# Hybrid decoder step: gathers of 4 picks for 32 tokens, and a weighted sum on four 32-column groups of TensorE

## The chip, the cores and the metric

One core of a Trainium2 chip. The metric is the device time of one execution in microseconds; the unchanged kernel takes 5937.07 us (median of 3 runs).

## The reference, cut to what matters

One layer: three gated branches, then a mixer of experts ("PEER"). The change touches the mixer alone. For every token (1024 of the prompt, 32 of the sample) and each of 8 heads, two sets of 128 keys are scored, the best 16 of each are combined to 256 candidates, and the best 16 of these name 16 of 16384 experts:

```
eidx = take_along_axis(cidx, pos, axis=-1)                 # (token, head, 16)
gw   = softmax(sc, axis=-1)
hpre = einsum('td,thkd->thk', xb, u_tab[eidx])             # a dot of 1024 with a gathered row
act  = gelu(hpre) * gw
y    = h + einsum('thk,thkd->td', act, v_tab[eidx])        # weighted sum of gathered rows
```

All is float32. An expert's u row and v row lie side by side in a scratch table, so one fetch of 8 KB brings both.

## The kernel before, in words

The stages run one after another; `experts` (line 2014) is the last and takes from 3160 us to the end. It works in 9 tiles: 8 of 128 prompt tokens and one of the 32 sample tokens. A turn is one head of a tile (for the sample tile 4 heads lie side by side on the partitions, so it has 2 turns); there are 66 turns of 16 picks, 1056 picks in all.

For one pick of a prompt tile, partition p holds token p:

- GpSimd (line 2133) issues one indirect DMA: for each of 128 partitions a row of 8 KB by the index in `E`, 1 MB in all, into one of 12 slots of `rows`. It waits for `v_done`, that the weighted sum has freed the slot 12 picks before.
- VectorE, `dot` (L2307), multiplies the u half by the tile's `n2u` and sums it. After each pick it does one of 16 parts of `route` for the turn after next: the top-16 searches, with `E` at part 13 (L2290) and the gates at part 15 (L2297).
- ScalarE, `weights` and `diagonal`: gelu (L2169), times gate (L2173), and a 128 x 128 diagonal of the weights (L2181).
- TensorE, `sum_row` (L2385): two products, diagonal by 512 columns of the v half, added up in PSUM (`ps_y`, 128 x 1024, double buffered by tile). Each float32 product is two pairs of weight load and matmul in the trace. At a tile's first pick the row `h` is put in by a product with the identity (L2379).
- TensorE also does the queries of the turn 3 ahead (L2354, after pick 4), its scores (L2367, after pick 7), and transposes at a tile's start.
- SyncE loads at each tile boundary `n2r` (L2114), `n2u` (L2103, double buffered by tile; for the sample tile 4 copies of 32 rows, L2106) and `h` (L2117), and stores `yo` (L2120). Its queue works in order: a wait holds all behind it.

In the sample tile a pick's 128 rows are 4 heads of 32 tokens; `fold` (128 x 32: the identity's four blocks added) times the weights takes the diagonal's place (L2185), so that the product has 32 output rows.

Of the kernel before, what the change touches and what calls it, by code (L numbers as in the profile page):

```python
# [23 lines left out]
P = 128  # L24
D = 1024
# [1988 lines left out]
def experts(nc, d):  # L2014
# [10 lines left out]
    SLOTS = 12  # L2025
    DIAGS = 4
    LOW = -3e38

    with ExitStack() as ctx:
# [16 lines left out]
        E, gates = sb("E", [P, 4, K], u32), sb("gates", [P, 4, K])  # L2046
# [3 lines left out]
        ps_q, ps_s = pb("ps_q", [P, 512]), pb("ps_s", [P, 512])  # L2050
# [4 lines left out]
        n2u_in = [sem(f"n2u_in{i}") for i in range(2)]  # L2055
# [5 lines left out]
        E_done, ex_in, ex_out, er_done, gate_done = (sem(n) for n in ("E", "ex_in", "ex_out", "er", "gate"))  # L2061
# [22 lines left out]

        def tokens(tile):
            return slice(tile * P, tile * P + width(tile))

        @block.sync
        def _(sp):
# [9 lines left out]
            def load_u(tile):  # L2099
                if tile >= 2:  # L2100
                    sp.wait_ge(dot_done, K * first_of(tile - 1))
                if tile < NT:
                    sp.dma_start(n2u[:, tile % 2], d["n2"][tokens(tile), :]).then_inc(n2u_in[tile % 2], 16)  # L2103
                else:
                    for i in range(PACK):
                        sp.dma_start(n2u[i * NS:(i + 1) * NS, tile % 2], d["n2"][tokens(tile), :]).then_inc(n2u_in[tile % 2], 16)  # L2106

            load_u(0)
            sp.dma_start(h[:], d["h"][tokens(0), :]).then_inc(h_in, 16)
            for tile in range(TILES):  # L2110
                n = width(tile)
# [25 lines left out]
        def _(act):  # L2137
# [28 lines left out]
            def weights(turn, k):  # L2166
# [3 lines left out]
                if k == 0:  # L2170
                    act.wait_ge(gate_done, turn + 1)
                act.wait_ge(gel_done, p + 1)
                nc.scalar.mul(w[:, j, k:k + 1], gel[:, j, k:k + 1], gates[:, turn % 4, k:k + 1]).then_inc(w_done, 1)  # L2173

            def diagonal(turn, k):
# [4 lines left out]
                if turn < NT * PH:  # L2180
                    nc.scalar.mul(diag[:, p % DIAGS, :], ident[:], w[:, j, k:k + 1]).then_inc(diag_done, 1)  # L2181
                else:
                    if p == NT * PH * K:
                        act.wait_ge(fold_done, PACK)
                    nc.scalar.mul(diag[:, p % DIAGS, 0:NS], fold[:], w[:, j, k:k + 1]).then_inc(diag_done, 1)  # L2185

            def outputs(tile):
                act.wait_ge(y_sum, tile + 1)
                if tile:
                    act.wait_ge(y_stored, 16 * tile)  # L2190
                n = width(tile)
                nc.scalar.copy(yo[0:n], ps_y[0:n, tile % 2]).then_inc(y_done, 1)
# [8 lines left out]
            for turn in range(TURNS):  # L2201
                for k in range(K):
                    weights(turn, k)
                    diagonal(turn, k)
                    if turn + 3 < TURNS:
                        if k == 2 and opens(turn + 3):
# [5 lines left out]
                    if k == 3 and turn and closes(turn - 1):  # L2212
                        outputs(tile_of(turn - 1))
# [282 lines left out]
```

## Time and profile before

| | |
|---|---|
| runs | 5933.24, 5937.07, 5937.49 us; median 5937.07 |
| profiled execution | 5942.84 us, its span 5941.2 us |
| mean granted TensorE clock | 0.882 of full |
| busy: TensorE matmul, VectorE, ScalarE, GpSimd | 4848.2, 2600.4, 1804.7, 1595.2 us |
| DMA | 1640.60 MB, mean 276 GB/s; 406 to 421 GB/s in most of the experts stage |

The span runs from the first to the last instruction; 1.6 us of the execution lie around it. A line of the profile gives line, engine and operation, output<-inputs, count, and then busy us and mean ns of one. Matmul ends are modelled, so a matmul's mean (613 ns) can be longer than the distance from one to the next. Times in brackets are idle time before an instruction and what ended it.

### The profile page before, as it was taken

How to read it: one execution, taken by the hardware profiler on the slowest of the kernel's cores; microseconds unless marked ns; L12 is line 12 of the kernel's file. 1: busy time of each engine (PE TensorE's matmuls, PEld its weight loads, DVE VectorE, ACT ScalarE, POOL GpSimd, SP SyncE). 2: the span in 40 equal slices, each digit the busy share in tenths (PEclk: the TensorE clock that was granted, in tenths of full speed). 3: DMA queues.
4: the chain of work that ended last, by engine and by line, in shares of the span. 5: the costliest groups of instructions: out<-in, count | busy, mean ns of one | idle time of the engine just before them, and what ended most of it. 6: DMA issues, size and time to landing. Idle time of an engine off the chain costs nothing. (4 is left out here: it accounts for less than half of the span.)

```text
span 5941.2 us, 55349 instructions
## 1 busy us (share of the span) xinstructions
PE 4848.2 (82%) x17762; PEld 3079.4 (52%) x17762; DVE 2600.4 (44%) x5524; ACT 1804.7 (30%) x4697; POOL 1595.2 (27%) x1401
## 2 busy tenths in 40 slices
PE   7999999956644448987996888888888888888898
PEld 6888888856544338983433333333333333333353
DVE  2111111146344432102224666666666666666664
ACT  3111111123223221102222444444444444444433
POOL 0000000025334301001002444444444434444433
PEclk9999999965566565558998999999999999999989
DMA  7989888711132322235216999999999999999988
GB/s 251 298 272 307 270 281 268 235 62 56 57 98 83 87 59 110 101 124 218 95 55 274 421 421 421 421 421 421 420 419 416 416 416 411 418 414 414 406 356 355
DMA packets 315418, 1640.60 MB, mean 276 GB/s; under 512 B 41240, under 2 KB 85912, under 8 KB 173272
## 3 DMA queue, kind: packets, MB, share of 16 engines
q0 software_dynamic: 167344, 1179.45, 48.7%
q1 hardware_dynamic: 112416, 236.91, 11.8%
q10 hardware_dynamic: 35456, 221.91, 11.5%
q8 instruction: 83, 1.36, 0.1%
q14 instruction: 119, 0.97, 0.0%
HBM read 1551.85 MB, written 315.93 MB: 314 GB/s over the span
## 5 line engine op out<-in xcount | busy, mean ns | idle before, releaser
L2385 PE MATMUL ex_ps_y<-ex_rows,ex_diag 128*128 128x512 f32 (+1 forms) x4224 | 2028.3, 613 | 402.1 <-ACT ex_diag L2181 383.4
L2307 DVE CUSTOM_DVE_ANT_0 ex_rows<-ex_rows,ex_n2u 128x1024 f32<-128x1024 f32 x1056 | 1294.5, 1226 | 940.8 <-DMA ex_rows<-scratch_uv,ex_E 931.0
L2133 POOL DMA_INDIRECT ex_rows<-scratch_uv,ex_E x1056 | 1157.8, 1096 | 1723.1 <-PE ex_ps_y L2385 1493.4
L2385 PEld LDWEIGHTS ex_ps_y<-ex_rows,ex_diag 128*128 128x128 f32 (+1 forms) x4224 | 729.2, 188 | 1604.0 <-ACT ex_diag L2181 939.7
L307 PE MATMUL pj_ps<-pj_w_hi,pj_nT 128*128 128x470 f32 (+1 forms) x3456 | 784.2, 378 | 22.1 <-PE pj_ps L307 14.0
L307 PEld LDWEIGHTS pj_ps<-pj_w_hi,pj_nT 128*128 128x128 f32 (+1 forms) x3456 | 622.1, 181 | 149.5 <-issue 32.0
L2169 ACT ACTIVATE ex_gel<-ex_dots 128x1 f32<-128x1 f32 x1056 | 213.8, 202 | 1366.2 <-DVE ex_dots L2307 1365.1
L211 DVE COPY pj_zo<-pj_ps 128x470 f32<-128x470 f32 (+1 forms) x108 | 69.7, 645 | 897.6 <-PE pj_ps L307 752.8
L2181 ACT ACTIVATE ex_diag<-ex_ident,ex_w 128x128 f32<-128x128 f32 x1024 | 411.0, 401 | 50.8 <-PE ex_ps_y L2385 17.9
L307 PE MATMUL pj_ps<-pj_w_lo,pj_nT 128*128 128x470 f32 (+1 forms) x1728 | 406.3, 377 | 0.0
L211 ACT COPY pj_zo<-pj_ps 128x470 f32<-128x470 f32 (+1 forms) x108 | 59.6, 552 | 996.8 <-PE pj_ps L307 622.7
L307 PEld LDWEIGHTS pj_ps<-pj_w_lo,pj_nT 128*128 128x128 f32 (+1 forms) x1728 | 312.2, 181 | 58.6
L2173 ACT ACTIVATE ex_w<-ex_gel,ex_gates 128x1 f32<-128x1 f32 x1056 | 311.1, 295 | 38.5 <-ACT ex_gel L2169 0.4
L2354 PEld LDWEIGHTS ex_ps_q<-ex_n2T,ex_wq 128*128 128x128 f32 x2304 | 288.8, 205 | 34.2 <-issue 30.1
L166 POOL DMA_DIRECT2D pj_w<-in_w_in x24 | 21.4, 893 | 1059.8 <-DVE pj_w_lo L199 1006.5
L2354 PE MATMUL ex_ps_q<-ex_n2T,ex_wq 128*128 128x128 f32 (+1 forms) x2304 | 289.4, 287 | 3.5 <-DMA ex_wq<-in_peer_wq 2.4
L1983 PE MATMUL mg_ps_b<-mg_wb,mg_aT 128*128 128x512 f32 (+1 forms) x576 | 259.8, 613 | 9.7 <-ACT mg_aT L1873 9.7
L1309 PE MATMUL at_ps_t<-at_ident,at_y 128*128 128x128 f32 x224 | 52.3, 405 | 188.8 <-DVE at_y L1239 175.0
L1983 PEld LDWEIGHTS mg_ps_b<-mg_wb,mg_aT 128*128 128x128 f32 (+1 forms) x576 | 107.0, 187 | 157.3 <-issue 153.9
L667 PE MATMUL gl_ps_a<-gl_qs,gl_kx 128*128 128x16 f32 x512 | 113.5, 375 | 91.7 <-POOL gl_kx L478 90.7
L667 PEld LDWEIGHTS gl_ps_a<-gl_qs,gl_kx 128*128 128x128 f32 x512 | 111.0, 331 | 96.8 <-POOL gl_kx L478 76.0
L1636 PEld LDWEIGHTS de_ps<-de_qb,de_kT 128*128 128x128 f32 x704 | 159.6, 333 | 2.2 <-DVE de_kT L1512 1.3
(362 smaller groups left out, 4651.0 us busy)
## 6 DMA issues: line engine op xcount, KB each, us to landing
pj_w<-in_w_in POOLq DMA_DIRECT2D x24, 1880.0 KB, 14.2
scratch_z<-pj_zo SPq DMA_DIRECT2D x192, 235.0 KB, 8.7
scratch_uv<-in_peer_u ACTq DMA_DIRECT2D x8, 4096.0 KB, 21.2
scratch_uv<-in_peer_v ACTq DMA_DIRECT2D x8, 4096.0 KB, 38.9
scratch_uv<-in_peer_u ACTq DMA_DIRECT2D x4, 8192.0 KB, 37.7
scratch_uv<-in_peer_v ACTq DMA_DIRECT2D x4, 8192.0 KB, 69.0
out_dk_s<-in_cache_dil_k ACTq DMA_DIRECT2D x8, 4088.0 KB, 44.4
out_dv_s<-in_cache_dil_v ACTq DMA_DIRECT2D x8, 4088.0 KB, 56.3
```

The lines of the kernel that those rows point to most:

```text
L211: copy(zo[0:n, s % BANKS, 0:CW], ps[0:n, s % BANKS, 0:CW]).then_inc(bank_out[s % BANKS], 1)
L307: last = nc.tensor.matmul(out, rows(a, k), weights(b, k), start=(m == 0 and k == 0), stop=(m == 2 and k == KD - 1))
L667: last = nc.tensor.matmul(ps_a[:, h, s * SUB:(s + 1) * SUB], kx[:, h, s, :], qs[:, h, s * SUB:(s + 1) * SUB], start=True, stop=True)
L1636: last = nc.tensor.matmul(ps_b[j][:, g, h * T + t:h * T + t + cols], kT[:, n % 2, h, :], qb[:, j, min(g, NG), h, t:t + cols], start=True, ...
L1983: last = nc.tensor.matmul(ps_b[0:n, q % 2], aT[:, k, 0:n], wb[:, k, 512 * c:512 * c + 512], start=(k == k0), stop=(k == k1 - 1))
L2133: pool.indirect_dma_start(out=rows[:, p % SLOTS, :], out_offset=None, in_=d["uv"], in_offset=bass.IndirectOffsetOnAxis(ap=E[:, turn % 4, k ...
L2169: nc.scalar.activation(gel[:, j, k:k + 1], dots[:, j, k:k + 1], ACT.Gelu).then_inc(gel_done, 1)
L2173: nc.scalar.mul(w[:, j, k:k + 1], gel[:, j, k:k + 1], gates[:, turn % 4, k:k + 1]).then_inc(w_done, 1)
L2181: nc.scalar.mul(diag[:, p % DIAGS, :], ident[:], w[:, j, k:k + 1]).then_inc(diag_done, 1)
L2307: nc.vector.tensor_tensor_reduce(out=row, in0=row, in1=n2u[:, tile % 2], scale=1.0, scalar=0.0, op0=ALU.mult, op1=ALU.add, accum_out=dots[ ...
L2354: last = nc.tensor.matmul(ps_q[:, at:at + n], wq[:, k, head * 256 + c * P:head * 256 + (c + 1) * P], n2T[:, k, 0:n], start=(k == 0), stop= ...
L2385: last = nc.tensor.matmul(y[0:n, 512 * c:512 * c + 512], diag[:, p % DIAGS, 0:n], rows[:, p % SLOTS, D + 512 * c:D + 512 * c + 512], start ...
```

## The change

A gather's partition 32j + t now holds token t of a group g of 32 tokens, and the j-th of 4 successive picks of the head. Pick k of a turn belongs to group k % 4 and covers picks 4q to 4q + 3 with q = k // 4, so a turn still has 16 gathers of 128 rows. The sample tile's gathers are unchanged. What follows from that:

- Indices and gates, computed token by token (`own`), are spread onto the new partitions: TensorE copies them 4 times by a product (`spread_picks`), VectorE takes 8 pieces out of PSUM (`take_spread`) and converts the indices.
- `n2u` holds, for each group, its 32 rows four times over; it is no longer double buffered: each group's four loads of 32 x 4 KB wait for the last dot of that group in the tile before.
- The weights' matrix is `fold` times weights (128 x 32) for all tiles, and the sum of a pick is 4 products of 256 columns whose outputs lie at partitions 0, 32, 64 and 96 (`ps_y[c * NS:(c + 1) * NS, g]`): column quarter c of the 1024 is at partitions 32c. `ps_y` is single buffered, and `h` and `yo` have the same layout; each is moved by 4 DMAs of 32 partitions, in pieces of 1 KB.
- 11 slots instead of 12.

```diff
-    SLOTS = 12
+    SLOTS = 11
     DIAGS = 4
+    G = P // NS
+    CW = D // G
...
+        copies4 = sb("copies4", [P, G, G, NS])
-        n2r, n2u, n2T = sb("n2r", [P, D]), sb("n2u", [P, 2, D]), sb("n2T", [P, KD, P])
-        h, yo = sb("h", [P, D]), sb("yo", [P, D])
+        n2r, n2u, n2T = sb("n2r", [P, D]), sb("n2u", [P, G, D]), sb("n2T", [P, KD, P])
+        h, yo = sb("h", [P, G, CW]), sb("yo", [P, G, CW])
-        diag = sb("diag", [P, DIAGS, P])
-        ps_y, ps_t = pb("ps_y", [P, 2, D]), pb("ps_t", [P, KD, P])
+        diag = sb("diag", [P, DIAGS, NS])
+        ps_y, ps_t = pb("ps_y", [P, G, CW]), pb("ps_t", [P, KD, P])
...
+        def by_column(a, tile):
+            rows32 = a[tokens(tile), :] if tile is not None else a
+            return rows32.rearrange("(g t) (c e) -> c t g e", t=NS, c=G)
...
+            def load_u(tile, g):
+                if tile:
+                    turn = first_of(tile) - 1
+                    sp.wait_ge(dot_done, K * turn + 3 * G + g + 1)
+                for j in range(G):
+                    sp.dma_start(n2u[j * NS:(j + 1) * NS, g], d["n2"][tile * P + g * NS:tile * P + (g + 1) * NS, :]).then_inc(n2u_in[g], 16)
+            def load_h(tile):
+                n = width(tile) // NS
+                for c in range(G):
+                    sp.dma_start(h[c * NS:(c + 1) * NS, 0:n], by_column(d["h"], tile)[c]).then_inc(h_in, 16)
+            for g in range(G):
+                load_u(0, g)
+            load_h(0)
             for tile in range(TILES):
                 if tile + 1 < TILES:
                     sp.wait_ge(n2_t, tile + 1)
                     sp.dma_start(n2r[0:width(tile + 1)], d["n2"][tokens(tile + 1), :]).then_inc(n2r_in, 16)
-                    load_u(tile + 1)
                     sp.wait_ge(h_used, tile + 1)
-                    sp.dma_start(h[0:width(tile + 1)], d["h"][tokens(tile + 1), :]).then_inc(h_in, 16)
+                    load_h(tile + 1)
+                    for g in range(width(tile + 1) // NS):
+                        load_u(tile + 1, g)
                 sp.wait_ge(y_done, tile + 1)
-                sp.dma_start(y, yo[0:n]).then_inc(y_stored, 16)
+                for c in range(G):
+                    sp.dma_start(y[c], yo[c * NS:(c + 1) * NS, 0:n]).then_inc(y_stored, 16)
...
-                    nc.scalar.mul(diag[:, p % DIAGS, :], ident[:], w[:, j, k:k + 1]).then_inc(diag_done, 1)
+                nc.scalar.mul(diag[:, p % DIAGS, :], fold[:], w[:, j, k:k + 1]).then_inc(diag_done, 1)
...
+            def take_spread(turn):
+                dve.wait_ge(r_done, turn + 1)
+                src = ps_r[:].rearrange("p (g c q j) -> p g c q j", g=G, c=2 * G, q=G)
+                for j in range(G):
+                    at = slice(j * NS, (j + 1) * NS)
+                    into = spread[at, turn % 4].rearrange("p c (q g) -> p g c q", g=G)
+                    for c in range(2):
+                        nc.vector.tensor_copy(into[:, :, c], src[at, :, c, :, j]).then_inc(spread_done, 1)
+                dve.wait_ge(spread_done, 2 * G * (turn + 1))
+                nc.vector.tensor_copy(E[:, turn % 4], spread[:, turn % 4, 0]).then_inc(E_done, 1)
...
             for turn in range(TURNS):
                 for k in range(K):
                     dot(turn, k)
+                    if k == 2 and turn + 1 < NT * PH:
+                        take_spread(turn + 1)
...
+            def spread_picks(turn):
+                for g in range(G):
+                    last = nc.tensor.matmul(ps_r[:, P * g:P * g + 2 * K], copies4[:, g].rearrange("p j t -> p (j t)"),
+                                            own[:, turn % 2].rearrange("p c k -> p (c k)"), start=True, stop=True)
+                last.then_inc(r_done, 1)
...
-                for c in range(2):
-                    last = nc.tensor.matmul(y[0:n, 512 * c:512 * c + 512], diag[:, p % DIAGS, 0:n],
-                                            rows[:, p % SLOTS, D + 512 * c:D + 512 * c + 512],
+                for c in range(G):
+                    last = nc.tensor.matmul(ps_y[c * NS:(c + 1) * NS, g], diag[:, p % DIAGS, :], rows[:, p % SLOTS, D + CW * c:D + CW * (c + 1)],
                                             start=False, stop=end, skip_group_check=True)
                 last.then_inc(v_done, 1)
...
+                    if k == 1 and turn + 1 < NT * PH:
+                        spread_picks(turn + 1)
```

ScalarE copies a finished tile out of `ps_y` before the next tile's first weights (before: after its pick 3), and TensorE waits for that copy before it begins the next tile's sum.

## Rows read from the trace of the kernel before

**Rows 1.** Windows of 100 us: engines' busy us (instructions), TensorE clock, DMA share, GB/s.

```profile
3400.00:3500.00 100.00, 84.31 (x239) 36.39 (x237) 66.40 (x173) 43.34 (x132) 43.12 (x40) 1.00 1.01 421
...
5700.00:5800.00 100.00, 94.90 (x365) 63.48 (x363) 60.11 (x147) 27.72 (x92) 31.48 (x29) 0.81 0.79 324
...
5800.00:5900.00 100.00, 89.34 (x224) 33.72 (x223) 50.61 (x108) 42.63 (x140) 47.72 (x44) 0.95 0.90 368
```

**Rows 2.** Groups by line and form, experts stage (3100 to 5941 us).

```profile
L2385 PE MATMUL ex_ps_y<-ex_rows,ex_diag 128*128 128x512 f32 x4096 | 1967.7, 613 | 383.8 <-ACT ex_diag L2181 383.4
...
L2307 DVE CUSTOM_DVE_ANT_0 ex_rows<-ex_rows,ex_n2u 128x1024 f32<-128x1024 f32 x1056 | 1294.5, 1226 | 940.8 <-DMA ex_rows<-scratch_uv,ex_E 931.0 <-issue 9.6
...
L2290 DVE SCALAR_TENSOR_TENSOR ex_E<-ex_picked 128x16 uint32<-128x16 f32 x66 | 11.3, 172 | 0.1
```

**Rows 3.** Waits from 3300 us on: total us, times, longest.

```profile
POOL ex_rows L2133 <- PE ex_ps_y L2385: 1452.9, 927, 25.0
...
DVE ex_rows L2307 <- DMA ex_rows<-scratch_uv,ex_E: 902.8, 1007, 3.5
```

**Rows 4.** Timeline of VectorE, dots at the boundary from tile 1 to 2.

```profile
3871.85 1.23 DVE L2307 CUSTOM_DVE_ANT_0 ex_rows<-ex_rows,ex_n2u 128x1024 f32<-128x1024 f32 x1 [0.84 <-DMA ex_rows<-scratch_uv,ex_E]
...
3889.35 1.23 DVE L2307 CUSTOM_DVE_ANT_0 ex_rows<-ex_rows,ex_n2u 128x1024 f32<-128x1024 f32 x1 [2.12 <-DMA ex_rows<-scratch_uv,ex_E]
...
3891.82 1.23 DVE L2307 CUSTOM_DVE_ANT_0 ex_rows<-ex_rows,ex_n2u 128x1024 f32<-128x1024 f32 x1 [0.63 <-DMA ex_rows<-scratch_uv,ex_E]
```

**Rows 5.** DMA issues by line: KB each, median us from issue to landing.

```profile
ex_rows<-scratch_uv,ex_E POOLq DMA_INDIRECT x1056, 25.3
...
ex_n2r<-scratch_n SPq DMA_DIRECT2D x8, 512.0 KB, 11.8
...
ex_n2u<-scratch_n SPq DMA_DIRECT2D x8, 512.0 KB, 15.2
...
ex_h<-scratch_h SPq DMA_DIRECT2D x8, 512.0 KB, 18.5
...
out_y_prompt<-ex_yo SPq DMA_DIRECT2D x8, 512.0 KB, 8.2
...
ex_n2u<-scratch_n SPq DMA_DIRECT2D x4, 128.0 KB, 13.3
```

**Rows 6.** Instructions of tile ex_rows: ns min/median/max, first and last start us.

```profile
L2307 DVE CUSTOM_DVE_ANT_0 ex_rows<-ex_rows,ex_n2u x1056: 1214/1226/1292, 3208.3 to 5932.7; 128x1024 f32<-128x1024 f32 x176
```

**Rows 7.** Timeline of VectorE, dots at that boundary.

```profile
5516.66 1.23 DVE L2307 CUSTOM_DVE_ANT_0 ex_rows<-ex_rows,ex_n2u 128x1024 f32<-128x1024 f32 x1 [0.83 <-DMA ex_rows<-scratch_uv,ex_E]
...
5528.69 1.23 DVE L2307 CUSTOM_DVE_ANT_0 ex_rows<-ex_rows,ex_n2u 128x1024 f32<-128x1024 f32 x1 [3.46 <-DMA ex_rows<-scratch_uv,ex_E]
...
5535.83 1.23 DVE L2307 CUSTOM_DVE_ANT_0 ex_rows<-ex_rows,ex_n2u 128x1024 f32<-128x1024 f32 x1 [1.33 <-DMA ex_rows<-scratch_uv,ex_E]
```

**Rows 8.** Windows of 5 us, one at each of two boundaries.

```profile
5190.00:5195.00 5.00, 5.00 (x35) 4.04 (x35) 2.10 (x5) 1.49 (x5) 0.94 (x1) 1.00 1.01 423
...
5525.00:5530.00 5.00, 2.87 (x10) 1.28 (x8) 1.54 (x6) 0.70 (x3) 2.40 (x3) 1.00 1.02 283
```

**Rows 9.** Timeline of GpSimd: the first gather.

```profile
3199.97 1.06 POOL L2133 DMA_INDIRECT ex_rows<-scratch_uv,ex_E  x1 [172.58 <-DVE ex_E L2290]
```

**Rows 10.** Page, part 3: queues, packets, MB, share of 16 engines.

```profile
q1 hardware_dynamic: 112416, 236.91, 11.8%
...
q8 instruction: 83, 1.36, 0.1%
```

**Rows 11.** Timeline of TensorE: one turn's queries.

```profile
3545.56 3.73 PE L2354 MATMUL ex_ps_q<-ex_n2T,ex_wq 128*128 128x128 f32 x32
```

**Rows 12.** Timeline of GpSimd: the gathers after two long pauses.

```profile
5756.10 0.94 POOL L2133 DMA_INDIRECT ex_rows<-scratch_uv,ex_E  x1 [25.00 <-PE ex_ps_y L2385]
...
5809.69 0.94 POOL L2133 DMA_INDIRECT ex_rows<-scratch_uv,ex_E  x1 [24.92 <-PE ex_ps_y L2385]
```

**Rows 13.** Chain that ended last, 5800 to 5870 us: start, us, what.

```profile
5813.88 32.83 PE ex_ps_y L2385 x76
```

More of the change, by code:

```diff
@@ L2054, in experts @@
         n2r_in, h_in, y_stored = sem("n2r_in"), sem("h_in"), sem("y_stored")
-        n2u_in = [sem(f"n2u_in{i}") for i in range(2)]
+        n2u_in = [sem(f"n2u_in{g}") for g in range(G)]
+        copies4_done, r_done, spread_done = sem("copies4"), sem("r"), sem("spread")
         n2_t, n2T_out, h_used, y_sum, y_done = sem("n2_t"), sem("n2T_out"), sem("h_used"), sem("y_sum"), sem("y_done")
@@ L2083, in width, with group @@
             return P if tile < NT else NS
+        def group(turn, k):
+            return k % G if turn < NT * PH else 0
+        def by_column(a, tile):
+            rows32 = a[tokens(tile), :] if tile is not None else a
+            return rows32.rearrange("(g t) (c e) -> c t g e", t=NS, c=G)
         def tokens(tile):
@@ L2097, in _ @@
             sp.dma_start(wq[:, :, 256:], wq_dram[:, :, 256:]).then_inc(wq_in, 16)
[L2099 to L2109, printed above, removed]
+            def load_u(tile, g):
[11 more added lines that the diff above has]
+            load_h(0)
             for tile in range(TILES):
-                n = width(tile)
+                n = width(tile) // NS
                 if tile + 1 < TILES:
@@ L2179, in diagonal @@
                     act.wait_ge(v_done, p - DIAGS + 1)
-                if turn < NT * PH:
-                    nc.scalar.mul(diag[:, p % DIAGS, :], ident[:], w[:, j, k:k + 1]).then_inc(diag_done, 1)
[L2182 to L2185, printed above, removed]
+                if p == 0:
+                    act.wait_ge(fold_done, PACK)
+                nc.scalar.mul(diag[:, p % DIAGS, :], fold[:], w[:, j, k:k + 1]).then_inc(diag_done, 1)
             def outputs(tile):
@@ L2189, in outputs @@
                 if tile:
[L2190 to L2192 removed]
+                    act.wait_ge(y_stored, 16 * G * tile)
+                n = width(tile) // NS
+                nc.scalar.copy(yo[:, 0:n], ps_y[:, 0:n]).then_inc(y_done, 1)
             for turn in range(3):
@@ L2202, in _ @@
                 for k in range(K):
+                    if k == 0 and turn and closes(turn - 1):
+                        outputs(tile_of(turn - 1))
                     weights(turn, k)
@@ L2205, in _ @@
                     if turn + 3 < TURNS:
-                        if k == 2 and opens(turn + 3):
+                        if k == 3 and opens(turn + 3):
                             turned_rows(turn + 3)
@@ L2224, in _ @@
                 nc.vector.tensor_tensor(fold[:], fold[:], ident[:, i * NS:(i + 1) * NS], ALU.add).then_inc(fold_done, 1)
+            nc.vector.tensor_copy(copies4[:], ident[:].rearrange("p (g t) -> p g t", g=G).unsqueeze(2).to_broadcast([P, G, G, NS])).then_inc(copies4_done, 1)
             def route(turn, part):
-                s, e, g = sc[:, turn % 2], E[:, turn % 4], gates[:, turn % 4]
+                s = sc[:, turn % 2]
+                mine = own[:, turn % 2] if turn < NT * PH else spread[:, turn % 4]
                 flat = cand[:].rearrange("p a b -> p (a b)")
@@ L2289, in route @@
                     dve.wait_ge(pick_done, turn + 1)
-                    nc.vector.scalar_tensor_tensor(out=e, in0=picked[:, 0], scalar=float(NKEY), in1=picked[:, 1],
-                                                   op0=ALU.mult, op1=ALU.add).then_inc(E_done, 1)
+                    if turn >= 2 and turn < NT * PH:
+                        dve.wait_ge(r_done, turn - 1)
+                    into, done = (mine[:, 0], own_done) if turn < NT * PH else (E[:, turn % 4], E_done)
+                    nc.vector.scalar_tensor_tensor(out=into, in0=picked[:, 0], scalar=float(NKEY), in1=picked[:, 1],
+                                                   op0=ALU.mult, op1=ALU.add).then_inc(done, 1)
                 elif part == 14:
@@ L2306, in dot @@
                 row = rows[:, p % SLOTS, 0:D]
-                nc.vector.tensor_tensor_reduce(out=row, in0=row, in1=n2u[:, tile % 2], scale=1.0, scalar=0.0, op0=ALU.mult,
+                nc.vector.tensor_tensor_reduce(out=row, in0=row, in1=n2u[:, g], scale=1.0, scalar=0.0, op0=ALU.mult,
                                                op1=ALU.add, accum_out=dots[:, turn % 2, k:k + 1]).then_inc(dot_done, 1)
@@ L2312, in _ @@
                     route(turn, part)
+                if turn == 0:
+                    take_spread(0)
             for turn in range(TURNS):
@@ L2395, in _ @@
                     turn_rows(turn)
+                if turn == 2:
+                    spread_picks(0)
                 queries(turn)
```

49 lines of the change are left out of this document (28 added, 21 removed).

## The prediction

> **What bounds the kernel now.** I read first the windows of 100 us: in the first window shown, one of two dozen like it, the DMA share is 1.01 and the rate 421 GB/s [rows 1], while VectorE is busy two thirds and ScalarE under a half of the time. TensorE's matmuls show 84%, but a busy matmul is modelled; its true pace is in the chain of waits where it had a backlog: 76 pieces in 32.83 us, 0.432 us each, four to a pick, 1.73 us [rows 13]. The dots follow each other at 2.48 us (3889.35 to 3891.82) [rows 4]: 1 MB (1048576 bytes) at 421 GB/s is 2.49 us. The waits say the same: VectorE sits 902.8 us for gathers to land. GpSimd's 1452.9 us for TensorE look like a rival bound, but are the wait for a free slot [rows 3], and a gather takes 25.3 us from issue to landing [rows 5], ten times its 2.49 us: about ten gathers are always under way, and a slot freed sooner only makes that queue longer. So a pick costs its bytes, and what TensorE does in 1.73 us is covered.
>
> What else moves in that stage costs time directly. At a boundary between prompt tiles SyncE moves n2r, n2u, h and the output, 512 KB each [rows 5], 2 MB. There five steps from dot to dot, 3871.85 to 3889.35, take 17.50 us [rows 4] in place of 5 x 2.484 = 12.42: 5.1 us more, and 2 MB at 421 GB/s are 5.0 us. These loads reach all 128 partitions and cost just their bytes.
>
> One boundary is unlike them: before the sample tile, n2r, four n2u copies and h are loads of 32 partitions, 128 KB each, six in all, after the 512 KB output. Five steps of the dots take 19.17 us there (5516.66 to 5535.83) [rows 7]: 6.75 us more, for 1.25 MB that would be 3.1 us by their bytes. Less 1.24 us for the output, six loads cost 5.5 us: **0.92 us each**, three times their 0.31 us. A window of 5 us in that burst moves 283 GB/s at a share of 1.02, one in the other kind of burst 423 GB/s [rows 8]: the engines were occupied, not idle, and moved less.
>
> By the Trainium skill (SBUF — State Buffer, Door 1: The DMA port swizzle), 32 neighbouring partitions are reached through 8 of the 16 ports, so such a load gets half the bandwidth; the trace agrees in direction, with 283 GB/s against 423.
>
> **The change, part by part** (against the profiled execution of 5942.84 us, 5.8 us over the median of the runs).
>
> *Gathers:* 1056 x 1 MB as before, same rows of 8 KB: 0. Cover: none is needed, the bytes are the same.
>
> *n2u:* four groups x four loads of 128 KB and 32 partitions per tile, 2 MB in place of 0.5 MB: 16 loads. *h:* four loads of 128 KB and 32 partitions. Bounds for one load: 0.31 us, its bytes, and 0.92 us as above; I take 0.92, because the nearest rows are of the same load, from the same table into the same buffer [rows 5, 7]. 20 x 0.92 = 18.4 us. *n2r:* 1.24 us, as before. *Output:* four stores of 128 KB out of 32 partitions. No row shows such a store beside gathers; by bytes 1.24 us, at 0.92 each 3.7 us. I take 1.24, since a store reads SBUF where gathers write it. Sum 20.9 us per boundary, less the 5.0 of now: +15.9 us. There are 7 boundaries from prompt tile to prompt tile: **+111 us**.
>
> *Pieces of 1 KB* in h and output: 768 more packets per tile. A packet of queue 1 took 0.118 x 5941 x 16 / 112416 = 0.100 us for 2.1 KB on the mean [rows 10], one of 8 KB 2.484/8 = 0.31 us; the line through both leaves 0.027 us per packet. 768 x 0.027 / 16 = 1.3 us per tile at most, over 8 tiles 10; at least 0. The 2.1 KB mean mixes queues under load, so I take 4.
>
> *The boundary before the sample tile* has its six loads of 32 partitions already; its h comes in four smaller ones and the output in four: +1 us.
>
> *Start:* the first gather goes out at 3199.97, when `E` is there [rows 9]. Now the gates (two parts of route), four small products, eight copies and the conversion lie ahead of it: nine VectorE instructions at about 172 ns [rows 2] are 1.5 us, the rest some 2 us: +3.5. The 16 n2u loads and four h loads at the start move 1.5 MB more, behind the last weights and beside the first gathers: 0 to 8 us; I take 2. Together **+5.5**.
>
> *VectorE* per turn: nine more small instructions, about 1.5 us, and a wait in which dots are queued behind TensorE's sum of pick 1 and the spreading products; some 2 us more. It idles 940.8 us in the stage, 14 us per turn [rows 2], and ten gathers ahead cover it: 0. If that cover were gone it would be 66 x 3.5 = 230 us.
>
> *ScalarE:* its diagonal of 128 columns becomes 32: less, and covered: 0. Its copy of the finished tile before the next tile's first weights holds up a few picks, covered by the same ten gathers.
>
> *TensorE:* eight pieces of 256 columns per pick. If nothing overlaps, bound by the queries, where 32 pieces of 128 columns with full weight loads took 3.73 us, 0.117 each [rows 11]: 8 x 2 x 0.117 = 1.87 us per pick; if the four groups run side by side, a quarter of 1.73, 0.43. A turn is then at most 30 + 5 = 35 us against 40 of DMA: covered either way, 0. If it idles more, its clock may go to the lower level; side by side a pick would still be under 1 us.
>
> *End:* the sample tile's queries hold TensorE for two pauses in the gathers of 25.00 and 24.92 us [rows 12], and the share falls to 0.79 and 0.90 in two windows, some 33 us of DMA time against 1.01 [rows 1]. With one slot less the queue is dry 2.5 us sooner, twice: +5. Faster sums would free slots sooner after each pause and leave no backlog ahead of the second: down to -10. I take 0.
>
> *Code:* TensorE gets 16 instructions per pick in place of 8, 8448 more. Queue 8 brings instructions, 83 packets of 16 KB now [rows 10]. If they serve TensorE alone, whose 35524 instructions (the page's two counts of 17762) make 428 per packet, that is 20 more; I take up to 40. Each is 16 KB on one of 16 engines, twice an 8 KB packet's 0.31 us or somewhat more: 0 if they fall where an engine has slack, 40 if all fell on the slowest engine at 1 us. The nearest observation is that steps of 2.48 us follow each other undisturbed, so +3.
>
> Sum: 111 + 4 + 1 + 5.5 + 0 + 3 = **+124 us**. 5942.84 + 124 = 6067; against the median of the runs 5937 + 124 = **6061 us**, 2.1% slower.
>
> By the Trainium skill's own figures (SBUF — State Buffer, the port table, 8 ports of 27.2 GB/s) a load of 128 KB takes an estimated 0.60 us; the sum by it would be near the second case below. The trace's 0.92 us is for the same thing and goes first.
>
> **The rivals.**
>
> *Twice the bytes.* The burst of rows 7 may hold something else besides (a block of code, the wait for a slot), and a 32-partition load costs 0.62 us, twice its bytes, since half of the destinations take it. Then a boundary costs 12.4 + 2.5 - 5.0 = +9.9 us, 69 in all, and the time is 5937 + 69 + 13.5 = 6019. For it: four copies in turn reach all partitions. Against: the measured 5.5 us.
>
> *Bytes only.* Twenty such loads spread over a longer stretch, between which the queue recovers, cost 0.31 each: +3.7 per boundary, 26 in all, 5937 + 26 + 13.5 = 5977. Against: the burst at 283 GB/s.
>
> *Late loads.* The four-fold n2u is single buffered: group g's loads are sent after its last dot and needed four picks later, 10 us at the normal pace, while such loads landed 13.3 us after issue [rows 5] in a queue. VectorE then stands some 5 us per group, and if that eats up the ten gathers, a boundary costs up to 10 us more: 7 x 10 = 70, 6131. It decides only when the standstill passes the 25 us under way; I see 5 to 15.
>
> *The release of slots is the bound* (the other side): if GpSimd's 1452.9 us for TensorE [rows 3] do set the pace of gathers, a shorter sum brings all steps to 2.484 us. 1056 x 2.484 = 2623 us against 2724 us from the first dot (3208.3) to the last (5932.7) [rows 6] leaves 101 us at most, of which 40 us are SyncE's bytes; a gain of 61 and no more, and with loads by bytes (+40) the kernel would end near 5916. It decides if the DMA share in long windows is under 1 at 2.5 us per pick; it is 1.01. Nearly excluded.
>
> *The groups don't run side by side* is a case of not doing what it says; it changes TensorE's pace from 0.43 to 1.87 us and the time by no more than the 15 us at the end.
>
> **How the numbers follow.** Forecast (0.8 to 1.0 us per load, 6040 to 6080): 0.58. Twice the bytes (6000 to 6035): 0.20. Bytes only (5965 to 5990): 0.08. Late loads (6085 to 6140): 0.08. Within 0.2%, which is about what a measurement of this kernel can tell from no change (12 us): 0.03, a mixture of cheap loads and a better end. Faster: 0.03. The range, 5990 to 6095, leaves out most of the bytes-only case, half of the late loads and both small cases; the likeliest case's own range is 6040 to 6080.
>
> **What would show it.** Right: at a boundary the dots stand 4 to 5 us apart for some ten picks, with the share at 1.0 and under 350 GB/s; between boundaries they keep 2.48 us; n2u issues are 132 in place of 12, and queue 1 moves about 12 MB more; a gather still lands 22 to 25 us after issue; TensorE waits for diagonals for most of a pick, and the first gather goes out 3 to 4 us later. Wrong: bursts at 420 GB/s (bytes only); dots waiting for n2u with the share under 0.9 (late loads); any change of the 2.48 us between boundaries, which would mean that not the bytes but something TensorE or GpSimd does sets the pace.

## The result and the profile after

| | median us | lowest to highest | ratio to before, 95% interval |
|---|---|---|---|
| before, on the same chip | 5935.15 | 5932.17 to 5937.49 (4 runs) | |
| after | 6046.24 | 6041.01 to 6048.01 (4 runs) | 1.0186, 1.0168 to 1.0204 |

The changed kernel is 111 us slower; +124 us, to 6061, had been forecast. Its page, with the busy times, the granted clock in 40 slices, and three of the queues (packets, MB, share of 16 engines):

```profile
span 6039.3 us, 65699 instructions
...
PE 4111.6 (68%) x22496; PEld 2801.9 (46%) x22496; DVE 2667.4 (44%) x6101; ACT 1719.3 (28%) x4697; POOL 1535.0 (25%) x1401
...
PEclk9999999966566565559986556556556656556565
...
q1 hardware_dynamic: 124608, 249.50, 12.5%
...
q8 instruction: 120, 1.97, 0.1%
```

TensorE is the engine that the change relieved, and it shows: 4112 busy us in place of 4848, and a clock of 0.5 to 0.6 in the experts stage, where it had been near full. Windows of 100 us (columns as in rows 1):

```profile
3300.00:3400.00 100.00, 57.91 (x452) 28.53 (x452) 69.78 (x187) 43.17 (x139) 39.18 (x40) 0.64 1.01 421
3500.00:3600.00 100.00, 49.54 (x348) 22.00 (x348) 56.47 (x155) 33.98 (x109) 33.45 (x32) 0.59 1.02 381
3800.00:3900.00 100.00, 52.16 (x364) 23.66 (x358) 61.80 (x177) 35.47 (x115) 35.84 (x34) 0.59 1.02 385
5800.00:5900.00 100.00, 81.09 (x500) 63.88 (x492) 60.21 (x162) 24.91 (x88) 28.42 (x26) 0.55 0.76 314
5900.00:6000.00 100.00, 47.12 (x384) 11.63 (x383) 51.52 (x109) 41.64 (x140) 46.92 (x44) 0.55 0.97 390
```

Away from a boundary nothing has changed: a share of 1.01 and 421 GB/s, as in [rows 1]. A window that holds a boundary between tiles (the second and third row) has the same share and moves 40 GB/s less. So the DMA engines are as occupied as ever and deliver less. Windows of 5 us place it:

```profile
3520.00:3525.00 5.00, 2.16 (x16) 0.40 (x16) 3.19 (x7) 1.64 (x6) 1.91 (x3) 0.50 1.02 424
3525.00:3530.00 5.00, 2.17 (x16) 0.41 (x16) 1.31 (x3) 1.14 (x4) 1.91 (x3) 0.50 1.03 318
3530.00:3535.00 5.00, 1.08 (x8) 0.20 (x8) 1.38 (x3) 1.77 (x4) 1.00 (x2) 0.50 1.02 290
3535.00:3540.00 5.00, 4.76 (x12) 1.38 (x12) 1.63 (x4) 0.88 (x4) 0.13 (x1) 0.50 1.02 288
...
3550.00:3555.00 5.00, 0.13 (x4) 0.00 (x0) 2.08 (x8) 0.74 (x3) 0.94 (x1) 0.50 1.00 383
3555.00:3560.00 5.00, 3.95 (x24) 2.26 (x25) 4.79 (x14) 1.71 (x7) 1.89 (x2) 0.50 1.02 421
3560.00:3565.00 5.00, 4.75 (x46) 3.90 (x48) 2.13 (x8) 1.91 (x7) 0.10 (x1) 0.86 1.01 417
```

SyncE's queue in the same stretch (start, us, what it issues):

```profile
3521.95 11.62 SPq L2118 DMA_DIRECT2D ex_n2u<-scratch_n  x16
3535.08 1.76 SPq L2140 DMA_DIRECT2D out_y_prompt<-ex_yo  x4
3536.89 0.43 SPq L2132 DMA_DIRECT2D ex_n2r<-scratch_n  x1
3538.99 9.93 SPq L2123 DMA_DIRECT2D ex_h<-scratch_h  x4
```

These rows show when SyncE issues, not when the bytes move: on the median a load of `h` lands 35.2 us after its issue, one of `n2u` 15.1 (DMA rows below). The rate from 3521 to 3585 us, in 40 slices of 1.6 us:

```profile
GB/s 420 415 430 310 297 305 274 315 279 274 305 256 323 289 277 328 312 317 293 420 417 415 428 426 421 405 424 428 382 353 360 343 371 348 365 349 399 410 415 420
```

It falls twice. From 3526 to 3551 us the 16 narrow loads of `n2u` move. Then come the four narrow stores and the wide load of `n2r`, and for 14 us the rate is back at 405 to 428 GB/s: a store out of 32 partitions slows nothing down. From 3566 to 3580 us, where the four loads of `h` land (32 to 38 us after their issue), it is at 343 to 382. Each queue's packets, MB and share of the 16 engines from 3530 to 3540 us, here and then in a_all_wide, a kernel of the experiments whose `n2u` loads of that stretch are wide:

```profile
q0 software_dynamic: 289, 2.11, 75.2%
q1 hardware_dynamic: 288, 0.79, 26.7%
```

```profile
q0 software_dynamic: 385, 2.80, 67.7%
q1 hardware_dynamic: 381, 1.37, 34.0%
```

Queue 0 has the gathers, queue 1 SyncE's loads. From bytes and shares, a gather's row of 8 KB occupied an engine for 0.47 us beside narrow loads and 0.32 beside wide ones, a load's row of 4 KB for 0.22 and 0.16. So the gathers pay for a narrow load too. VectorE's dots there:

```profile
3525.66 1.22 DVE L2342 CUSTOM_DVE_ANT_0 ex_rows<-ex_rows,ex_n2u 128x1024 f32<-128x1024 f32 x1 [1.17 <-DMA ex_rows<-scratch_uv,ex_E]
3530.60 1.22 DVE L2342 CUSTOM_DVE_ANT_0 ex_rows<-ex_rows,ex_n2u 128x1024 f32<-128x1024 f32 x1 [3.63 <-DMA ex_rows<-scratch_uv,ex_E]
...
3540.50 1.23 DVE L2342 CUSTOM_DVE_ANT_0 ex_rows<-ex_rows,ex_n2u 128x1024 f32<-128x1024 f32 x1 [3.26 <-issue]
3546.85 1.22 DVE L2342 CUSTOM_DVE_ANT_0 ex_rows<-ex_rows,ex_n2u 128x1024 f32<-128x1024 f32 x1 [4.07 <-DMA ex_n2u<-scratch_n]
3552.92 1.22 DVE L2342 CUSTOM_DVE_ANT_0 ex_rows<-ex_rows,ex_n2u 128x1024 f32<-128x1024 f32 x1 [3.05 <-DMA ex_n2u<-scratch_n]
3554.93 1.22 DVE L2342 CUSTOM_DVE_ANT_0 ex_rows<-ex_rows,ex_n2u 128x1024 f32<-128x1024 f32 x1
3556.50 1.27 DVE L2342 CUSTOM_DVE_ANT_0 ex_rows<-ex_rows,ex_n2u 128x1024 f32<-128x1024 f32 x1
...
3582.09 1.23 DVE L2342 CUSTOM_DVE_ANT_0 ex_rows<-ex_rows,ex_n2u 128x1024 f32<-128x1024 f32 x1 [0.85 <-DMA ex_rows<-scratch_uv,ex_E]
```

From 3525.66 to 3582.09 are 15 steps: 56.4 us where 15 x 2.484 are 37.3. The boundary costs 19.2 us against 5.1 in [rows 4], 14.1 more. Twice the dot waited for `n2u`, 4.07 and 3.05 us, and the next three followed at 1.6 to 2.3 us, faster than gathers come: that delay was caught up.

Waits from 3300 us on, which answer to [rows 3], and DMA issues, which answer to [rows 5]:

```profile
POOL ex_rows L2153 <- PE ex_ps_y L2436: 1567.9, 774, 27.7
PE ex_ps_y L2436 <- ACT ex_diag L2204: 1193.4, 763, 6.3
DVE ex_rows L2342 <- DMA ex_rows<-scratch_uv,ex_E: 771.7, 789, 4.1
DVE ex_rows L2342 <- DMA ex_n2u<-scratch_n: 57.8, 16, 4.4
```

```profile
ex_n2u<-scratch_n SPq DMA_DIRECT2D x132, 128.0 KB, 15.1
ex_rows<-scratch_uv,ex_E POOLq DMA_INDIRECT x1056, 23.7
ex_n2r<-scratch_n SPq DMA_DIRECT2D x8, 512.0 KB, 31.6
ex_h<-scratch_h SPq DMA_DIRECT2D x32, 128.0 KB, 35.2
out_y_prompt<-ex_yo SPq DMA_DIRECT2D x32, 128.0 KB, 23.6
```

GpSimd still waits longest for TensorE (1567.9 us), although TensorE itself now waits 1193.4 us for weights. Such a wait names who frees the slot, not what is slow. What answers to [rows 2] and [rows 6], and to [rows 11] (queries) and [rows 13] (a backlog of TensorE), in three views:

```profile
L2436 PE MATMUL ex_ps_y<-ex_rows,ex_diag 128*32 128x256 f32 x8448 | 999.4, 567 | 1234.9 <-ACT ex_diag L2204 1232.9
```

```profile
L2342 DVE CUSTOM_DVE_ANT_0 ex_rows<-ex_rows,ex_n2u x1056: 1201/1225/1296, 3205.6 to 6031.4; 128x1024 f32<-128x1024 f32 x176
```

```profile
3644.82 6.37 PE L2393 MATMUL ex_ps_q<-ex_n2T,ex_wq 128*128 128x128 f32 x32
3651.12 1.07 PE L2436 MATMUL ex_ps_y<-ex_rows,ex_diag 128*32 128x256 f32 x16
...
5901.12 2.79 PE L2436 MATMUL ex_ps_y<-ex_rows,ex_diag 128*32 128x256 f32 x24
...
5908.07 4.51 PE L2436 MATMUL ex_ps_y<-ex_rows,ex_diag 128*32 128x256 f32 x48 [0.40 <-ACT ex_diag L2204]
```

First dot to last dot takes 2825.8 us against 2724.4, 101.4 more. The sums are read from TensorE's backlogs. At a granted clock of 1.00, two picks behind the queries (16 pieces) took 1.07 us, at most 0.54 a pick. At 0.50, three picks (24 pieces) took 2.56 us until the next product began, 0.85 a pick. Before, it was 1.73 us at 1.00. The 48 pieces at 5908 us, also at 1.00, are no backlog of TensorE: six picks in 4.51 us is the pace of ScalarE, which was busy 4.06 us of them and needs three instructions for a pick's weights. The queries pay for the clock: 6.37 us, nearly all at 0.50, in place of 3.73 at 1.00.

The time is placed by a measure that every kernel here has: the mean distance between the output stores of the eight prompt tiles, over the six intervals before the sample tile, **328.8 us per tile before and 343.3 after**, +14.5. These six boundaries make 87.2 us of the 101.4. The seventh, into the last prompt tile, costs only 9.7 more, counted from the 65th dot of one tile to the 65th of the next: it is the burst of [rows 7], which was dear before (6.75 us), and its `n2r` and `h` are the sample tile's and small in both kernels. The rest is 1.8 us up to the first tile's 65th dot and 2.7 us from that of the last prompt tile on, with the sample tile in it. Before the first dot, from the load of the keys to the first gather, it is 42.5 us against 38.7. The remaining 6 us of the difference of medians are not placed; with the same stages ahead of it, the first gather went out at 3199.97 us in the kernel before and at 3195.05 in b_11slots, so two executions differ by nearly as much.

### The profile page after: what moved, and what is told of

Same layout as the page of the kernel before. It is cut to its first block and busy times, and to the rows that moved or that the text cites. A ratio compares the mean times of both kernels' runs of the same rounds, so it can differ in the third digit from the quotient of the medians.

```text
span 6039.3 us, 65699 instructions
## 1 busy us (share of the span) xinstructions
PE 4111.6 (68%) x22496; PEld 2801.9 (46%) x22496; DVE 2667.4 (44%) x6101; ACT 1719.3 (28%) x4697; POOL 1535.0 (25%) x1401
## 3 DMA queue, kind: packets, MB, share of 16 engines
q14 instruction: 125, 1.02, 0.0%
## 5 line engine op out<-in xcount | busy, mean ns | idle before, releaser
L2436 PE MATMUL ex_ps_y<-ex_rows,ex_diag 128*32 128x256 f32 x8448 | 999.4, 567 | 1234.9 <-ACT ex_diag L2204 1232.9
L2153 POOL DMA_INDIRECT ex_rows<-scratch_uv,ex_E x1056 | 1098.4, 1040 | 1889.1 <-PE ex_ps_y L2436 1614.2
L2436 PEld LDWEIGHTS ex_ps_y<-ex_rows,ex_diag 128*32 128x32 f32 x8448 | 208.1, 132 | 1908.2 <-ACT ex_diag L2204 1878.6
L2393 PEld LDWEIGHTS ex_ps_q<-ex_n2T,ex_wq 128*128 128x128 f32 x2304 | 404.4, 277 | 55.8 <-issue 50.6
L2393 PE MATMUL ex_ps_q<-ex_n2T,ex_wq 128*128 128x128 f32 (+1 forms) x2304 | 416.9, 363 | 4.6 <-DMA ex_wq<-in_peer_wq 3.5
L2204 ACT ACTIVATE ex_diag<-ex_fold,ex_w 128x32 f32<-128x32 f32 x1056 | 339.3, 321 | 34.5
L2195 ACT ACTIVATE ex_w<-ex_gel,ex_spread 128x1 f32<-128x1 f32 x1056 | 311.3, 295 | 38.3
L199 DVE TENSOR_TENSOR pj_w_lo<-pj_w,pj_w_hi 128x3760 fp32r<-128x3760 f32 x28 | 114.0, 4071 | 96.8 <-ACT pj_w_hi L194 96.8
## 6 DMA issues: line engine op xcount, KB each, us to landing
scratch_uv<-in_peer_v ACTq DMA_DIRECT2D x8, 4096.0 KB, 37.3
```

The lines of the kernel that those rows point to most:

```text
L2153: pool.indirect_dma_start(out=rows[:, p % SLOTS, :], out_offset=None, in_=d["uv"], in_offset=bass.IndirectOffsetOnAxis(ap=E[:, turn % 4, k ...
L2195: nc.scalar.mul(w[:, j, k:k + 1], gel[:, j, k:k + 1], spread[:, turn % 4, 1, k:k + 1]).then_inc(w_done, 1)
L2204: nc.scalar.mul(diag[:, p % DIAGS, :], fold[:], w[:, j, k:k + 1]).then_inc(diag_done, 1)
L2393: last = nc.tensor.matmul(ps_q[:, at:at + n], wq[:, k, head * 256 + c * P:head * 256 + (c + 1) * P], n2T[:, k, 0:n], start=(k == 0), stop= ...
L2436: last = nc.tensor.matmul(ps_y[c * NS:(c + 1) * NS, g], diag[:, p % DIAGS, :], rows[:, p % SLOTS, D + CW * c:D + CW * (c + 1)], start=Fals ...
```

## The experiments

Theory: a boundary costs by how few partitions the loads of 128 KB reach. Rivals: by their bytes; by their number or their pieces of 1 KB; by what else changed (spreading, eight pieces per pick, the clock, 11 slots, the single-buffered `n2u`). "Per tile" is the mean of the six store to store distances.

| kernel | median us | ratio, 95% interval | per tile us |
|---|---|---|---|
| b_11slots | 5936.41 | 1.0005, 0.9995 to 1.0014 | 328.4 |
| b_11slots_wide1MB | 5954.93 | 1.0031, 1.0020 to 1.0043 | 331.0 |
| b_11slots_narrow1MB | 5987.28 | 1.0088, 1.0071 to 1.0105 | 335.1 |
| b_11slots_half1MB | 5983.47 | 1.0081, 1.0065 to 1.0098 | 334.9 |
| b_11slots_narrow1MB_swapped | 5983.30 | 1.0080, 1.0063 to 1.0096 | 335.1 |
| a_n2u_wide | 5988.03 | 1.0087, 1.0070 to 1.0103 | 335.2 |
| a_hy_wide | 6027.85 | 1.0159, 1.0142 to 1.0176 | 341.2 |
| a_hy_narrow_4KB | 6041.79 | 1.0183, 1.0166 to 1.0200 | 343.2 |
| a_all_wide | 5969.96 | 1.0062, 1.0046 to 1.0079 | 333.0 |
| b_split_queries | 5919.94 | 0.9973, 0.9963 to 0.9984 | 328.6 |
| b_split_no_n2r | 5912.69 | 0.9961, 0.9948 to 0.9975 | 327.3 |

### The kernel before with 11 slots, and loads added to it

b_11slots:

```diff
-    SLOTS = 12
+    SLOTS = 11
```

> The kernel before with 11 slots for the gathered rows in place of 12. Theory (bytes and the way to the partitions set the pace): about nine gathers of 2.49 us stay under way instead of ten, so the steps between dots keep 2.48 us and only the two pauses at the sample tile's queries cost 2.5 us each: +0 to +5 us. Rival (the depth of the queue is part of the loss): steps grow between boundaries too, +20 us or more.

The slot costs nothing that can be measured, and the freed memory holds a spare buffer `more` into which SyncE loads 1 MB per tile, eight times. Seven of these fall on a boundary; the first goes out at about 3183 us, ahead of the first gather. b_11slots_wide1MB does it in two loads of 128 partitions (waits and semaphores left out here):

```diff
+                sp.dma_start(more[:, i], d["n2"][0:P, :]).then_inc(more_in[i], 16)
```

> As b_11slots, and at each of 8 tile boundaries 1 MB more is loaded into a spare buffer by two loads of 128 partitions, 512 KB each. Both theories: by its bytes, 2.5 us per boundary, +20 us over b_11slots (15 to 25).

b_11slots_narrow1MB moves the same bytes in eight loads of 32 partitions:

```diff
+                for j in range(PACK):
+                    sp.dma_start(more[j * NS:(j + 1) * NS, i], d["n2"][j * NS:(j + 1) * NS, :]).then_inc(more_in[i], 16)
```

> As b_11slots_wide1MB, with the same 1 MB in eight loads of 32 partitions, 128 KB each. Theory (a load of 32 partitions costs two to three times its bytes): 8 x 0.62 to 0.92 = 5.0 to 7.4 us per boundary, +40 to +59 us over b_11slots, and windows of 5 us near 290 GB/s at full share. Rival (bytes only; what the changed kernel loses lies in its buffers and slots): +20 us as in the wide one.

The wide megabyte costs 2.6 us per tile (by its bytes 2.5), the narrow one 6.7. A narrow load costs 6.7 / 8 = 0.84 us. No engine computes with these loads' data or waits for it. Windows of 5 us with the added loads, the wide ones first, then the narrow ones:

```profile
3555.00:3560.00 5.00, 3.04 (x5) 0.69 (x4) 2.58 (x6) 2.54 (x6) 1.26 (x1) 0.83 1.02 420
3560.00:3565.00 5.00, 4.17 (x5) 1.58 (x6) 2.23 (x4) 1.61 (x6) 1.09 (x2) 0.50 1.03 422
```

```profile
3555.00:3560.00 5.00, 2.74 (x6) 1.16 (x7) 1.33 (x3) 4.00 (x8) 1.75 (x1) 1.00 1.02 302
3560.00:3565.00 5.00, 2.93 (x4) 0.83 (x3) 1.84 (x3) 0.90 (x3) 1.56 (x1) 0.51 1.02 285
```

At one share, 420 against 285 to 302 GB/s: the effect is in the kernel before, with only a slot less and the added loads. Two more kernels ask what makes a load narrow. b_11slots_half1MB takes four loads of 64 partitions:

```diff
+                for j in range(2):
+                    sp.dma_start(more[64 * j:64 * j + 64, i], d["n2"][64 * j:64 * j + 64, :]).then_inc(more_in[i], 16)
```

> As b_11slots_narrow1MB, with the 1 MB in four loads of 64 partitions and 256 KB (0 to 63, 64 to 127) in place of eight of 32. In that run a tile took 334.2 to 335.1 us from output to output, against 330.5 with wide loads. Theory (a load reaches half of the ways into SBUF whether it has 32 or 64 neighbouring partitions): as narrow, 334 to 335 us a tile, 5982 to 5990 us. Rival (the loss goes by the share of partitions left out, or by the number of DMAs): about half of it, 332.5 us a tile, near 5971 us. Third (loads of all kinds but the whole width alike lose nothing; only the small size does): 330.5, near 5955.

and b_11slots_narrow1MB_swapped sends the quarters in another order, so that neighbours in the queue lie in different halves of the partitions:

```diff
-                for j in range(PACK):
+                for j in (0, 2, 1, 3):
```

> As b_11slots_narrow1MB, with the four quarters of a buffer loaded in the order 0, 2, 1, 3 (partitions 0, 64, 32, 96), so that neighbours in the queue lie in different halves. If neighbouring loads are under way together, both halves of SBUF are written at a time and the loss falls by a third or more: 332 to 333 us a tile, near 5972 us. If each load is drained before the next, nothing changes: 334 to 335 us, 5982 to 5990 us. I expect the second.

Both stay at the price of the eight narrow loads, 6.5 and 6.7 us over b_11slots per tile. Half as many loads, each of twice the partitions, win nothing: neither the number of loads nor being 32 wide sets the price, and the order doesn't either. One rival is left: each wide load here has 512 KB and each narrow one 256 KB at most. No run sends a small load to all 128 partitions, so that a load's size, and not its partitions, sets the price is not excluded. For it, the price per byte would have to be the same at 128 and 256 KB and gone at 512; and the stores of 128 KB, which cost their bytes alone, don't show it. In the half-wide kernel the same window reads:

```profile
3555.00:3560.00 5.00, 1.98 (x4) 0.68 (x4) 1.29 (x4) 1.93 (x5) 2.34 (x2) 1.00 1.02 292
```

This is the rule of the Trainium skill (SBUF — State Buffer, Door 1: The DMA port swizzle), whose heading says that 64 partitions are about as fast as 32: a block of 64 partitions from 0 or 64 still reaches 8 of 16 ports. The trace agrees in that. By its 27.2 GB/s per port a load of 128 KB through 8 ports would take an estimated 0.60 us; the runs show 0.81 to 0.84, beside gathers. The same skill (DMA: Bandwidth & Descriptors, Back-pressure in remote DMA) says of transfers between cores that a saturated destination port also holds up a DMA engine's other queues. That would fit here, where the gathers slow down as well, but these transfers aren't of that kind, and no run shows the mechanism.

### The changed kernel with its loads made wide

a_n2u_wide:

```diff
-                for j in range(G):
-                    sp.dma_start(n2u[j * NS:(j + 1) * NS, g], d["n2"][tile * P + g * NS:tile * P + (g + 1) * NS, :]).then_inc(n2u_in[g], 16)
+                if tile < NT:
+                    sp.dma_start(n2u[:, g], d["n2"][tokens(tile), :]).then_inc(n2u_in[g], 16)
```

> The changed kernel; each group's n2u of a prompt tile is loaded by one load of 128 partitions and 512 KB (the tile's own rows, not the group's 32 rows four times, so the dots of prompt tiles after it are of other rows), in place of four of 32 partitions. Same bytes, same waits. Theory (partitions): a boundary's four groups fall from some 12 us to 5.0 us, -7 us per boundary, 7 to 8 boundaries, -50 us (-35 to -65). Rival (bytes, or the single buffering of n2u): no change within 10 us.

58 us of the 111 are gone, with the same bytes: 8.1 us per tile for 16 loads, 0.51 each above their 0.31 us, 0.82 in all. The edit also lets `n2u` land sooner; but the narrow loads that nothing waits for cost 0.84 each, so no part of the 8.1 us has to be put down to waiting.

a_hy_wide (one load of `h` and one store of the output, on 128 partitions with rows of 4 KB), and a_hy_narrow_4KB (four of each on 32 partitions, but with rows of 4 KB), of which this is the load:

```diff
-                for c in range(G):
-                    sp.dma_start(h[c * NS:(c + 1) * NS, 0:n], by_column(d["h"], tile)[c]).then_inc(h_in, 16)
+                if tile < NT:
+                    sp.dma_start(h[:].rearrange("p g e -> p (g e)"), d["h"][tokens(tile), :]).then_inc(h_in, 16)
```

```diff
-                    sp.dma_start(h[c * NS:(c + 1) * NS, 0:n], by_column(d["h"], tile)[c]).then_inc(h_in, 16)
+                    if tile < NT:
+                        sp.dma_start(h[c * NS:(c + 1) * NS].rearrange("p g e -> p (g e)"), d["h"][tile * P + c * NS:tile * P + (c + 1) * NS, :]).then_inc(h_in, 16)
```

> The changed kernel; a prompt tile's h and output go by one DMA of 128 partitions in rows of 4 KB each (the column-quarter order of h and of the output is left out, so the output's elements are misplaced), n2u stays narrow. Theory: with n2u wide, a tile takes 335.0 us from output to output against 328.0 + 3.7 of bytes, so h and output hold 3.3 us per boundary over their bytes: -3.3 x 8 = -26 us against the changed kernel (-15 to -35). Rival (the n2u loads are all of it): -5 us or less.

> The changed kernel; h and output still by four DMAs of 32 partitions, but in rows of 4 KB and not in pieces of 1 KB (order left out as in a_hy_wide). If the loss of h and output is one of partitions: within 8 us of the changed kernel. If it is one of the 1 KB pieces: as a_hy_wide, -15 to -35 us.

Wide, `h` and output save 2.1 us per tile, 18 us by the medians, less than expected. With longer rows but narrow they save 0.1: the pieces of 1 KB cost next to nothing, and partitions are what counts here too. Of these 2.1 us, four loads at 0.51 take all. That fits the trace of the changed kernel, where the rate was 421 GB/s while the stores moved and fell for `h`: the narrow stores cost their bytes alone.

a_all_wide makes both edits together.

> The changed kernel with n2u, h and output all by DMAs of 128 partitions in rows of 4 KB (contents left out as in a_n2u_wide and a_hy_wide). Theory: only the 1.5 MB more per tile is left, +3.7 us per boundary, 331.7 us per tile: 5937 + 26 + 8 = 5971 us (5960 to 5980). If a step between boundaries, TensorE's lower clock or the spreading cost something of their own, it stays above 5985.

The savings add up: 10.3 us per tile, where 8.1 and 2.1 were measured singly. The rate stays up while `n2u` is loaded, at a clock of 0.50 and of 0.88:

```profile
3530.00:3535.00 5.00, 2.86 (x10) 1.04 (x11) 1.64 (x5) 2.54 (x7) 0.94 (x1) 0.50 1.02 421
3535.00:3540.00 5.00, 3.76 (x27) 1.62 (x25) 2.28 (x10) 0.82 (x3) 1.54 (x2) 0.88 1.02 416
```

It is left 4.2 us per tile over the kernel before, and the 1.5 MB more of `n2u` are 3.7 us by their bytes. So spreading, eight pieces per pick, the lower clock (mean 0.702), 11 slots and the single-buffered `n2u` together have about 0.5 us per tile left to them. (No dot waits for `n2u` in this kernel, so it does not test late loads.)

### A version that is faster than both

The profile of before has two places without cover: the sample tile's queries, 128 pieces in one block, for which gathers pause 25 us [rows 12] and the share falls [rows 1], and the 512 KB load of `n2r`, whose rows `n2u` holds already. b_split_queries sends the sample's queries one head at a time (not shown here: the scores and ScalarE's copies move back with them):

```diff
+                        late = turn + 3 >= NT * PH
+                        if late and k in (3, 6, 9, 12):
+                            queries(turn + 3, k // 3 - 1)
-                        if k == 4:
+                        if k == 4 and not late:
```

> The kernel before; the sample tile's queries, which held TensorE for 25 us and stopped the gathers for 25.0 and 24.9 us, are issued one head at a time after picks 3, 6, 9 and 12, with their scores after pick 14. Theory (the only loss of DMA time that the stage has is there): both pauses go, -15 us (-10 to -20). Rival (the clock stays at its lower level, so that sums and queries together need over 40 us per turn): -5 us or less.

b_split_no_n2r has this and transposes from `n2u` (the first tile's `n2u` is then loaded first, where `n2r` was):

```diff
-                    sp.dma_start(n2r[0:width(tile + 1)], d["n2"][tokens(tile + 1), :]).then_inc(n2r_in, 16)
...
-                    last = nc.tensor.transpose(ps_t[:, k, 0:n], n2r[0:n, k * P:(k + 1) * P], ident[0:n, 0:n])
+                    last = nc.tensor.transpose(ps_t[:, k, 0:n], n2u[0:n, tile % 2, k * P:(k + 1) * P], ident[0:n, 0:n])
```

> As b_split_queries, and the tile's rows for the transposes are read from n2u, which holds the same rows, so that n2r's load of 512 KB goes. Theory (a boundary costs its bytes): -1.24 us per boundary and tile, -9 us more, -24 us in all against the kernel before (-17 to -30). Rival (loads at a boundary are hidden): as b_split_queries.

They take 5919.94 and 5912.69 us. In b_split_queries the longest pause of the gathers after 5600 us is 6.5 us, and the two windows that had 324 and 368 GB/s in [rows 1] now read:

```profile
5700.00:5800.00 100.00, 95.50 (x388) 55.24 (x387) 59.78 (x150) 36.82 (x113) 35.64 (x34) 0.91 0.94 365
5800.00:5900.00 100.00, 85.80 (x226) 27.03 (x225) 56.52 (x118) 40.77 (x137) 42.38 (x40) 1.00 1.01 412
```

Without `n2r` a tile takes 327.3 us in place of 328.6: 1.3 us, what 512 KB cost by their bytes. b_split_no_n2r is 0.39% faster than the kernel before (0.25 to 0.52%) and 134 us faster than the changed one.

## Why the prediction was right, step by step

- **The bound.** Right. Gathers kept 2.48 us between boundaries at 421 GB/s, with a TensorE that did a pick in 0.85 us at half the clock instead of 1.73 and GpSimd waiting for it even longer. The release of slots as the bound is out: all that relief bought nothing.
- **A load of 32 partitions, 0.92 us.** The mechanism and the place were right, the size was too high: 0.81 to 0.84 us in four kernels. The step that failed was to take the whole excess of the one burst in [rows 7], less the output, for six loads; 6 x 0.82 is 4.9 of those 5.5 us, so 0.6 us of that burst belonged to something else, which no run names. "Twice the bytes" (0.62) and "bytes only" (0.31) both fall. Whether a load's partitions or its size set the price is argued, not shown, as said above.
- **Per boundary, +15.9 us.** Measured +14.1 at one and +14.5 on the mean of six. With 0.82 for 0.92 the sum itself gives 20 x 0.82 + 1.24 + 1.24 - 5.0 = +13.9. Counting seven alike was a second slip: the burst of [rows 7] is not a boundary of its own before the sample tile but the seventh, when SyncE fetches the sample tile's rows ahead. It has 16 narrow loads more, but no full `n2r` and `h`, and started from 6.75 us: +9.7. Together 96.9 us for 111.
- **The output at its bytes.** Right, as the trace of the changed kernel shows (421 GB/s while the stores moved) and a_hy_wide bears out.
- **Pieces of 1 KB, +4 us.** About 1: the line through two mean packets overstated it, as its own reservation said.
- **Sample boundary +1, end 0, code +3.** The stage outside the seven boundaries took 4.5 us more (1.8 and 2.7), where these three and the pieces made 8; the runs don't separate them. The pauses grew to 27.7 and 26.8 us: the block of queries now runs at 0.50 throughout, 27.5 us, where before its first 3.3 us had 1.00 and it took 24.2 and 23.6. Yet the DMA time lost in the two windows fell from 33 to 29 us. Queue 8 moved 37 more packets where 20 to 40 had been worked out, without a cost that could be seen.
- **Start +5.5 us.** The first gather went out 3.8 us later, for 3.5 forecast. The 2 us for the loads beside it aren't visible. So the forecast is too high by 14 us in the boundaries and by 5 in these smaller terms, and 6 us that are not placed bring the measured time back towards it: that the total missed by only 13 owes something to luck.
- **VectorE, TensorE, ScalarE, clock: 0.** a_all_wide shows that all of them together cost about 0.5 us per tile. The four groups of TensorE do run side by side: at a clock of 1.00 a pick took at most 0.54 us where it took 1.73 before, and at 0.50 it took 0.85, twice the 0.43 of the prediction.
- **Late loads.** They happened, 57.8 us in 16 waits, but the gathers under way covered them: at the boundary shown the DMA share stays between 0.99 and 1.06 in every window of 5 us from 3520 to 3565, and the 0.82 us that a load of `n2u` costs is no more than the 0.84 of loads that nothing waits for.

## What to carry to other kernels

Where the DMA engines are the bound, cost a load by the partitions it reaches as well as by its bytes: beside gathers, one of 128 or 256 KB into 32 or 64 neighbouring partitions cost 2.6 times its bytes, partly through the gathers beside it, while a store out of 32 cost its bytes alone; one load of 128 partitions brought the same 512 KB for 1.24 us in place of 3.3. A faster engine that waits for data gives nothing back, and the wait that names it says nothing about its speed. Look for the places where the bounding resource is not full (here 25 us of pauses, and a load of rows already there): they brought the only gain.

## What the runs showed that was not expected

- Loads of 64 partitions cost as much per byte as loads of 32 (334.9 and 335.1 us per tile), and alternating halves in one queue doesn't help.
- A slower load slows its neighbours: at a share of 1.02 the total fell from 421 to 285 GB/s, and gathers, which reach all partitions, came 4.9 us apart in place of 2.48 while the narrow loads ran beside them (dots at 3525.66 and 3530.60). A gather's row of 8 KB took 0.47 us of an engine in place of 0.32.
- Stores out of 32 partitions don't: at 1.02 and 1.01 the rate was 421 and 417 GB/s (3555 to 3565 us), with pieces of 1 KB.
- TensorE's granted clock in the experts stage went from near 1.0 to 0.50 (1.2 in place of 2.4 GHz) in stretches where it was busy 2.16 us of 5 (3520 to 3525 us), and the kernel did not notice: a_all_wide at 0.702 on the mean fits its bytes to 0.5 us per tile.
